# Reordered chunk steps, early first mixing pass and unrolled halves in a hybrid DeltaNet decoder block on one core

## What is computed

```python
h = x
h = h + hybrid_mixer(rms_norm(h))          # 4 gated-DeltaNet heads | 8 short-conv groups -> w_out
h = h + memory_cross_attention(rms_norm(h), rms_norm(mem))   # 256 memory tokens, 4 heads
h = h + swiglu(rms_norm(h))                # d_ff 2816
return rms_norm(h)
```

```python
v_new = u - w @ state
o     = q_dec @ state + attn @ v_new
state = state * exp(g_last) + k_dec.T @ v_new
```

## Time and profile before

| | |
|---|---|
| median of 3 runs | 3297.31 us (3297.11 to 3297.98) |
| profiled execution, own time | 3298.23 us |
| its span | 3296.5 us, 41758 instructions |
| TensorE busy | 3128.1 us (95%) |
| VectorE, ScalarE, GpSimd busy | 1200.0, 957.2, 1004.4 us (36%, 29%, 30%) |
| mean granted clock of TensorE | 0.982 |

### The profile page before, as it was taken

One profiled execution on the slowest core, in us unless ns is written; L12 is line 12 of the kernel. 1 busy time (PEld: TensorE's weight loads), 2 busy tenths in 40 slices (PEclk: granted clock), 3 DMA queues, 4 the chain that ended last, 5 costly groups with the idle time before them and its releaser, 6 DMA issues.

```text
span 3296.5 us, 41758 instructions
## 1 busy us (share of the span) xinstructions
PE 3128.1 (95%) x14926; PEld 2572.2 (78%) x14926; DVE 1200.0 (36%) x1630; ACT 957.2 (29%) x1732; POOL 1004.4 (30%) x814
## 2 busy tenths in 40 slices
PE   7899899989999999999979989998999999999998
PEld 7787677768888888888867767776888788888887
DVE  1454455546342122112235545554634311221123
ACT  3522344424232111111143234442423311111112
POOL 6322333334213332233222223333412323322332
PEclk9899999999999999999989999999999999999999
DMA  6422222132101111111132222223211111111111
GB/s 227 170 93 99 77 75 64 45 141 84 45 20 52 51 47 54 38 51 51 57 122 71 102 86 65 64 64 125 72 54 33 58 39 51 46 55 38 51 51 70
DMA packets 108410, 235.31 MB, mean 71 GB/s; under 512 B 9296, under 2 KB 50320, under 8 KB 108304
## 3 DMA queue, kind: packets, MB, share of 16 engines
q1 hardware_dynamic: 45520, 163.14, 14.7%
q10 hardware_dynamic: 62784, 70.83, 6.3%
HBM read 191.96 MB, written 41.98 MB: 71 GB/s over the span
## 4 chain that ended last, share of the span: by engine, by line
issue 45%; PE 31%; POOL 14%; DVE 4%; ACT 3%; DMA 1%; POOLq 0%; DVEq 0%; ACTq 0%; SPq 0%
POOL w_lo L1546 8%; PE PS L1995 6%; PE PS L1997 6%; PE PS L1996 6%; POOL row_lo L441 3%; PE PS L1252 2%; PE PS L1274 1%; PE PS L1232 1%; POOL heads_lo L1554 1%; DVE xn L1848 1%; PE PS L1264 1%; PE PS L1370 1%; PE PS L1305 1%; PE PS L1374 1%; PE PS L1372 1%
## 5 line engine op out<-in xcount | busy, mean ns | idle before, releaser
L1995 PE MATMUL PS<-act_hi,w_hi 128*128 128x512 f32 (+1 forms) x2496 | 983.1, 394 | 16.6 <-ACT stage L487 6.9
L1997 PE MATMUL PS<-act_hi,w_lo 128*128 128x512 f32 (+1 forms) x2496 | 958.3, 384 | 0.0
L1996 PE MATMUL PS<-act_lo,w_hi 128*128 128x512 f32 (+1 forms) x2496 | 957.4, 384 | 0.0
L1546 POOL TENSOR_TENSOR w_lo<-raw,w_hi 128x1024 fp32r<-128x1024 f32 x204 | 494.0, 2435 | 493.2 <-ACT w_hi L1625 492.3
L1995 PEld LDWEIGHTS PS<-act_hi,w_hi 128*128 128x128 f32 x2496 | 473.7, 190 | 103.6 <-issue 20.5
L1997 PEld LDWEIGHTS PS<-act_hi,w_lo 128*128 128x128 f32 x2496 | 472.6, 189 | 92.1
L1996 PEld LDWEIGHTS PS<-act_lo,w_hi 128*128 128x128 f32 x2496 | 473.7, 190 | 83.2 <-issue 1.4
L1863 DVE TENSOR_TENSOR h<-h,PS 128x1024 f32<-128x1024 f32 x272 | 332.1, 1221 | 382.0 <-PE PS L2033 345.7
L441 POOL TENSOR_TENSOR row_lo<-aa,row_hi 128x512 fp32r<-128x512 f32 x88 | 113.7, 1292 | 913.3 <-ACT row_hi L826 913.3
L1176 DVE TENSOR_TENSOR aa<-sg,PS 128x512 f32<-128x512 f32 x88 | 60.6, 688 | 880.7 <-ACT sg L822 880.7
L2029 PE MATMUL PS<-w_hi,row_hi 128*128 128x512 f32 x832 | 324.7, 390 | 0.0
(11 more groups left out here) (262 smaller groups left out, 3886.9 us busy)
## 6 DMA issues: line engine op xcount, KB each, us to landing
raw<-in_w_units SPq DMA_DIRECT2D x220, 512.0 KB, 3.3
h<-in_x SPq DMA_DIRECT2D x16, 1024.0 KB, 8.5
qkvz_d<-stage ACTq DMA_DIRECT2D x64, 256.0 KB, 2.5
raw<-att_d SPq DMA_DIRECT2D x32, 512.0 KB, 3.3
prep_raw<-in_w_units SPq DMA_DIRECT2D x16, 512.0 KB, 4.6
att_d<-product ACTq DMA_DIRECT2D x16, 512.0 KB, 3.2
qk<-qkvz_d ACTq DMA_DIRECT2D x32, 256.0 KB, 2.9
out<-result ACTq DMA_DIRECT2D x16, 512.0 KB, 4.3
```

Source lines behind the costliest of these rows:

```text
L1546: pool.tensor_tensor(w_lo[slot][:, :], raw[raw_slot][:, :], w_hi[slot][:, :].bitcast(f32), ALU.subtract)\
L1995: nc.tensor.matmul(out_ap, whi, xhi, start=start, stop=False)
L1996: nc.tensor.matmul(out_ap, whi, xlo, start=False, stop=False)
L1997: return nc.tensor.matmul(out_ap, wlo, xhi, start=False, stop=stop)
```

## The change

It consists of these parts.

1. In the chunk: TensorE makes the products of `gram` before the transposes of v, and it is these transposes that now wait for the new state. The state product goes to bank 3 (that of the new values) and not to bank 5. `am0` is made of `gram` and of a masked decay that GpSimd prepares one chunk ahead (a third product in `decays_pool`), and no longer of A. VectorE's order changes: sum of `osq` before the state; four small operations of the output norm (`output_scale`) ahead of `gram`'s products; `vb` ahead of `Xm`; the scaled outputs behind `Xe`; the taps of the short convolution from y3 to y5 to x1, x3, x4, x5, x6. ScalarE makes `rms_estimate` before `sc_rms` and `ln_norms` of y6 before its other work of y6. `FILL` of the steps w, v, o goes from 1, 1, 0 to 2, 0, 0.
2. GpSimd's subtractions of 128x1024 in the recurrence (`sq_lo`, and `split_lo` at y3 and y6) are four instructions of 128x256 each.
3. End of a half: the first two rows of mixing are loaded in step y2 of the last chunk (to another place, `mix_first`), and rounded and subtracted right behind the last chunk. TensorE starts pass 0 without the last outputs; the sums of the short convolution and the transposes of the outputs stand in pass 0 behind tile 1. SyncE issues three of the four loads of h when the state product is done, the fourth when the last output is stored. VectorE adds tile 0 between the two last normalisations.
4. GpSimd, ScalarE, VectorE and TensorE have the two halves written out instead of a loop.

```diff
--- before.py
+++ after.py
...
-FILL = [0, 0, 2, 2] + [2, 1] * 6 + [1, 1, 0]
+FILL = [0, 0, 2, 2] + [2, 1] * 6 + [2, 0, 0]
...
-        mix_first = sb("mix_first", [P, 2, D], at=[act_lo_at])
+        mix_first = sb("mix_first", [P, 2, D], at=[229344 - 8192])
...
             pool.wait_ge(S["sqh_ready"], n + 1)
             pool.wait_ge(S["nrm_full"], n)
-            pool.tensor_tensor(sq_lo[:, :, :, :].rearrange("p a h t -> p (a h t)"),
-                               rn[:, :, :, :].rearrange("p a h t -> p (a h t)"),
-                               sq_hi[:, :, :, :].rearrange("p a h t -> p (a h t)").bitcast(f32),
-                               ALU.subtract).then_inc(S["sql_ready"], 1)
+            for a in range(2):
+                for hh in range(0, NH, 2):
+                    last = pool.tensor_tensor(hflat(sq_lo[:, a, hh:hh + 2, :]),
+                                              hflat(rn[:, a, hh:hh + 2, :]),
+                                              hflat(sq_hi[:, a, hh:hh + 2, :]).bitcast(f32),
+                                              ALU.subtract)
+            last.then_inc(S["sql_ready"], 1)
...
             pool.tensor_tensor(dec[par][:, 0, :, :], dec[par][:, 0, :, :], gate("beta", m),
+                               ALU.mult).then_inc(S["decm_ready"], 1)
+            pool.wait_ge(S["decm_ready"], n * 3 + 1)
+            pool.wait_ge(S["a1t_full"], n)
+            pool.tensor_tensor(am0[:, :, :], dec[par][:, 0, :, :], over_heads(first_mask[:, :]),
                                ALU.mult).then_inc(S["decm_ready"], 1)
...
-                    split_lo((n_u + 2, 2, 2) if par == 0 else (n_u + 4, 1, 1))
+                    split_lo((n_u + 2, 2, 2) if par == 0 else (n_u + 4, 1, 1), 4)
...
-                    split_lo((n_u + 3, 0, 0))
+                    split_lo((n_u + 3, 0, 0), 4)
...
                 if step == "gram":
                     if not first:
+                        rms_estimate(act, n - 1)
                         if par == 0:
                             sc_rms(act, R - 1, 0)
-                        rms_estimate(act, n - 1)
...
+                if step == "y6" and not last:
+                    ln_norms(act, n + 1)
...
+                if step == "y2" and last:
+
+                    act.wait_ge(S["y_stored"], (half * 8 + 6) * 16)
+                    for k in range(2):
+                        load_mix(act, half, k)
...
-            act.wait_ge(S["scy_ready0"], R + 1)
-            for k in range(2):
-                load_mix(act, half, k)
+            mix_hi(act, half, 0)
+            rms_estimate(act, half * TT + TT - 1)
             sc_rms(act, R, 0)
             sc_squares(act, R, 1)
-            rms_estimate(act, half * TT + TT - 1)
-            sc_rms(act, R, 1)
+            sc_rms(act, R, 1, 6)
...
+                    if not first:
+                        output_scale(dve, n - 1)
                     dve.wait_ge(S["gram_full"], n + 1)
-                    dve.wait_ge(S["decm_ready"], n * 2 + 2)
+                    dve.wait_ge(S["decm_ready"], n * 3 + 3)
+                    dve.tensor_tensor(two(am0[:, :, :]), gram[:, :, :, 0, :], two(am0[:, :, :]),
+                                      ALU.mult).then_inc(S["am0_ready"], 1)
                     dve.tensor_tensor(two(A[:, 0, :, :]), gram[:, :, :, 0, :], two(A[:, 0, :, :]),
                                       ALU.mult).then_inc(S["a_ready"], 1)
-                    dve.wait_ge(S["a_ready"], n + 1)
-                    dve.tensor_tensor(am0[:, :, :], A[:, 0, :, :], over_heads(first_mask[:, :]),
-                                      ALU.mult).then_inc(S["am0_ready"], 1)
                 if step == "a1t":
 
+                    dve.wait_ge(S["vt_full"], n + 1)
+                    dve.wait_ge(S["vn_full"], n)
+                    dve.tensor_tensor(vb[:, :, :], r4(bank(3)), gate("beta", m), ALU.mult)\
+                        .then_inc(S["vb_ready"], 1)
                     dve.wait_ge(S["a1t_full"], n + 1)
-                    dve.wait_ge(S["vn_full"], n)
...
-                    dve.wait_ge(S["vt_full"], n + 1)
-                    dve.tensor_tensor(vb[:, :, :], r4(bank(3)), gate("beta", m), ALU.mult)\
-                        .then_inc(S["vb_ready"], 1)
+                    if not first:
+                        outputs_scaled(dve, n - 1)
...
                         sc_y_product(dve, R - 1, 1)
                 if step == "y1":
-                    if not first:
-                        normalise_o(dve, n - 1)
...
-                if par == 1 and step in ("y3", "y4", "y5"):
-                    for i, c in {"y3": ((0, 0), (1, 0)), "y4": ((2, 0), (0, 1)),
-                                 "y5": ((1, 1), (2, 1))}[step]:
-                        sc_tap(dve, R, j, c, i)
-                if par == 1 and step == "y6":
+                if par == 1 and step in ("x1", "x3", "x4"):
+                    sc_tap(dve, R, j, 0, {"x1": 0, "x3": 1, "x4": 2}[step])
+                if par == 1 and step == "x5":
+                    sc_tap(dve, R, j, 1, 0)
+                    sc_tap(dve, R, j, 1, 1)
+                if par == 1 and step == "x6":
+                    sc_tap(dve, R, j, 1, 2)
...
+                    dve.wait_ge(S["osq_ready"], n + 1)
...
+
                     dve.wait_ge(S["kv_full"], n + 1)
                     dve.wait_ge(S["s_ready"], n * 4)
                     for hh in range(NH):
                         dve.scalar_tensor_tensor(
                             state[:, hh, :], state[:, hh, :],
                             G["elast"][:, bass.ds(m, 1), hh:hh + 1].rearrange("p n h -> p (n h)"),
-                            r4(bank(5))[:, hh, :], ALU.mult, ALU.add).then_inc(S["s_ready"], 1)
...
+                            r4(bank(3))[:, hh, :], ALU.mult, ALU.add).then_inc(S["s_ready"], 1)
+
+        def end_dve(dve, half, add):
             R = half * 4 + 3
             n = half * TT + TT - 1
             sc_y_product(dve, R, 1)
+            normalise_o(dve, n)
             sc_normalise(dve, R, 3, 0)
-            normalise_o(dve, n)
+            add(0)
             sc_normalise(dve, R, 3, 1)
...
-                pe.wait_ge(S["vnew_ready"], n)
-                for hh in range(NH):
-                    t = nc.tensor.transpose(r4(bank(3))[:, hh, :], vv[:, par, hh, :], ident[:, :])
-                t.then_inc(S["vt_full"], 1)
-                pe.wait_ge(S["s_ready"], n * 4)
                 for hh in range(NH):
                     t = nc.tensor.matmul(PS[:, 5 + hh // 2, (hh % 2) * 256:(hh % 2 + 1) * 256],
                                          kqn[:, hh, 0, :],
                                          kqn[:, hh, :, :].rearrange("p s t -> p (s t)"),
                                          start=True, stop=True)
                 t.then_inc(S["gram_full"], 1)
+                pe.wait_ge(S["s_ready"], n * 4)
+                for hh in range(NH):
+                    t = nc.tensor.transpose(r4(bank(3))[:, hh, :], vv[:, par, hh, :], ident[:, :])
+                t.then_inc(S["vt_full"], 1)
...
-                    t = nc.tensor.matmul(r4(bank(5))[:, hh, :], kdec[:, hh, :], vnew[:, hh, :],
+                    t = nc.tensor.matmul(r4(bank(3))[:, hh, :], kdec[:, hh, :], vnew[:, hh, :],
...
-                        sp.wait_ge(S["oo_ready"], (half + 1) * TT)
-                        sp.wait_ge(S["y_stored"], (half + 1) * 16 * 8)
-                        sp.wait_ge(S["o_stored"], (half + 1) * 16 * TT)
...
+                        sp.wait_ge(S["vnew_ready"], (half + 1) * TT)
+                        sp.wait_ge(S["kv_full"], (half + 1) * TT)
                         for k in range(TT // 2):
+                            if k == 3:
+
+                                sp.wait_ge(S["oo_ready"], (half + 1) * TT)
+                                sp.wait_ge(S["o_stored"], (half + 1) * 16 * TT)
...
+            def split_lo(n, pieces=1):
...
+                for i in range(pieces):
+                    cs = slice(i * D // pieces, (i + 1) * D // pieces)
+                    last = pool.tensor_tensor(w_lo[slot][:, cs], raw[raw_slot][:, cs],
+                                              w_hi[slot][:, cs].bitcast(f32), ALU.subtract)
+                last.then_inc(S["w_lo_ready"], 1)
...
-            with act.Fori(0, NHALF) as half:
+            for half in range(NHALF):
...
+                    if t % 2 == 0:
+                        dve.wait_ge(S[f"h_in{t // 2}"], (half + 1) * 32)
+                    row_add(t, half * ROW_PASSES)
+
+                end_dve(dve, half, first_add)
+                for t in range(1, TT):
...
-                sc_sums(pe, half * 4 + 3, 1)
-                pe.wait_ge(S["wt_ready"], n + 1)
-                transpose_o(pe, n)
-
-
-                pe.wait_ge(S["scyn_ready"], (half + 1) * 8)
-                pe.wait_ge(S["vnew_ready"], (half + 1) * TT)
...
+                def outputs_left():
+                    pe.wait_ge(S["attn_ready"], n + 1)
+                    sc_sums(pe, half * 4 + 3, 1, 6)
```

(70 more changed lines are left out.)

26 lines of the change are left out of this document (7 added, 19 removed).

## The result

The changed kernel takes 3253.57 us, the median of four runs (3247.91 to 3254.35), beside 3297.64 us of the kernel before on the same chip: ratio 0.9862, 95% interval 0.9845 to 0.9879. That is 44 us less. The profiled execution took 3253.67 us over a span of 3251.9 us.

The account below looks back on a forecast made before the run. The prediction held that order, not work, costs: TensorE waits on chains over mostly idle VectorE and ScalarE. Terms -20.6 - 5.9 + 2.4 + 4.8 - 5.2 = -24.5 us gave 3273 us, range 3254 to 3289.

Parts of the forecast that it names:

- the earlier logarithm: Ahead of w, even chunks and chunk 0: removes TensorE's wait, but only 0.2 of 0.8 us stays gained; -1.6 us.
- Front: First transposes to y1 takes 6.0 us: odd chunks gain 1.75 us, even 1.0, chunk 0 0.3; -20.6 us.
- rival D: Front of the chunk: VectorE is late, delaying transposes of v, `vb` and y1 by 1 us; 3287 us, chance 0.08.
- Pieces and taps: y1 to w: shorter waits for `Xe` and `Xm`, partly eaten by a later `sq_lo`; -7.0 us in the recurrence.
- Rival B: Recurrence: the pieces hurt, as GpSimd goes first or `sq_lo` comes late in even chunks too; 3282 us, chance 0.14.
- Output scaling out of y1: Step y1: moving the scaling of the outputs out was not counted as a gain; 0 us.
- Tail: w to o: a second slice costs +4.0 us, the logarithm made earlier gives -1.6; together +2.4 us.
- End of a half: Mixing: pass 0 starts 8.3 us earlier, but pass 1 waits for its rows and the clock drops; +4.8 us.
- Rival C: End of a half: early mixing pays, pass 1 following pass 0 without a stop; 3252 us, chance 0.16.
- Written out: Between the halves: straight code removes the wait for the program at the jump back; -5.2 us.
- Rival E: Small loops: at new addresses their jumps back wait for the fetch, +21 to +52 us; chance 0.06.
- Start of the recurrence: Start of each half: TensorE waits for `sq_lo` itself, now in pieces; +0.55 us twice, +1.1 us.

Follow-up runs that it names:

- the two-by-two: The changed kernel with whole subtractions (3262.06 us), with the taps at y3, y4, y5 again (3251.01 us), and with both undone (3262.41 us).
- whole_and_late: The changed kernel with GpSimd's subtractions whole again and the taps back at y3, y4, y5; 3262.41 us.
- pieces alone: The kernel before with only GpSimd's subtractions cut into four pieces; 3290.78 us, ratio 0.9969 to the kernel before.
- tail_one_one: The changed kernel with one slice behind w and one behind v again, in place of two and none; 3245.54 us.
- rows_earlier: The changed kernel with units 2 and 3 of the output projection loaded before h and the second mixing pass's rows loaded earlier; 3235.42 us.
- loop_halves: The changed kernel with the two halves as one loop again on the four engines; 3259.85 us.

## Why the forecast was right in direction and short in size

The steps that failed are terms 2, 3 and 4: pieces and taps were sized too small, the scaling of the outputs was put at nothing, and the earlier logarithm was held to be eaten up by the next wait.

1. **Front** (-20.6): measured -22.0. Right, mechanism and size: 5.82 us in place of the forecast 6.0, and 6.3 to 6.4 in chunk 0. By luck two slips cancel in part: chunk 1 was counted as gaining 1.75 us like the other odd ones, but its front took 6.94 us before and it gains 1.1, while chunk 0 gains 0.6 and not 0.3. The order on TensorE alone is 16 of it. VectorE keeps up, rival D is out.
2. **Pieces and taps** (-7.0 in the recurrence): the two-by-two gives -12.0 (586.8 - 574.8). The mechanism was right, the term too small by 5. The wait for `sq_lo` that was to eat half of the gain is 0.4 us and not 1.1, because GpSimd was held up less. An odd chunk gains 1.65 us and not 1.0 (y1 to w 23.9 us in whole_and_late, 22.25 here), and even chunks gain 0.15 where I had 0. In chunk 0, where I had +0.3, y4 to y6 took 8.45 us with whole subtractions and takes 8.34. Rival B is out: pieces alone are -9.9. The Trainium skill (SBUF — State Buffer, "SBUF: two separate sides") says that of the two engines the one that starts first holds the shared ports for a whole instruction. The trace agrees: the copy takes 1.51 us beside a whole subtraction and 0.57 beside pieces. By their durations VectorE had its turn behind one piece at most.
3. **Output scaling out of y1** (not counted, 0): -7. This is the step whose mechanism failed. I followed who waits for `vb`, `Xe` and `am`, and took the scaling for work off the path. The earlier trace rows does not name it; the full list of the same view has it once, in chunk 1:

```profile
PE PS L1274 <- DVE osq L961: 0.3, 1, 0.3
```

   The starts had it: y1 to y2 took 3.80 us in chunk 3 and y2 to y3, with the same work of TensorE, 3.44; and the code has the wait of x1.
4. **Tail** (+2.4): -0.8, three parts. The slice behind w costs the 0.5 us that were forecast, but in even chunks as well as in odd ones: +7.3, less 0.8 behind v. But the earlier logarithm gives back its whole 0.9 us in even chunks and chunk 0 (-7.3), where I took 0.2, supposing that the wait for `wt` would follow. The second slice covers that wait: in tail_one_one, without it, even chunks wait there and take the same time from w to o.
5. **End of a half** (+4.8): +3.5 by the traces against the kernel before, 5.1 when taken back (-7.1 us in time, with overlapping intervals). Right, chain and sign: "nothing of the 8.3 us arrives". (The start of pass 0 adds up to 686.2, not 686.4.) The arrival of unit 2 rested on an assumed latency of 2.8 us, which no run shows by itself; by it `split_hi` was to start 27.2 us behind the state product, and it started 26.9 us behind it. Rival C, early mixing pays, is out for this kernel, and is true of rows_earlier. That its time, 3252, is near the measured 3253.57 is chance: the gain came in the recurrence, and early mixing cost time.
6. **Written out** (-5.2): 5.3 for the jump, as forecast; the other 1.8 of the -7.1 are not the loop's, since loop_halves takes 929.6 us where the kernel before takes 931.4, and their cause is open. The written-out code of chunks 0 and 7, costed at nothing, is worth about 1 us a half. The Trainium skill (Runtime: NRT & Kernel Launch, "Instruction fetch mechanics") has a taken branch wait for a fetch where its target lies outside the fetched window. The trace agrees: 8.38 us of idle time ahead of the table load with the loop against 2.92 without. Rival E, small loops that pay for their new place, is out: chunk 3 starts without a gap. (Its count was off by one: 3273 with five such stops is already 3299.)
7. **Start of the recurrence** (+1.1): +2.8, of which 0.9 is the subtraction in pieces (2.77 us in place of 2.34, twice). In the first half, another 0.7 is a later load of q, k and v (ScalarE's first square comes 7.9 us behind the gates, 7.2 before), and the sums of squares behind the longer wait take 0.63 to 0.77 us each, before 0.40 to 0.63.

Terms 2, 3 and 4 hold 15 of the missing 20 us, the written-out chunks some 2. Another 2 are the clock granted in chunk 0 of the first half, which is luck. The rest are small sums of either sign, terms 1, 5, 6 and 7 and "everything else" of the table.

Left open: why chunk 0 is granted now the lower and now the full clock; why the same code up to the gates takes 351.4 to 353.9 us, and 1 to 2 us more between the first transposes and the gates of half 1 in most of the later kernels.

## What to carry to other kernels

A list of waits names only the last releaser, and shows no short ones. Before costing a moved instruction at nothing, look up every semaphore that it raises and whose write needs the bank or buffer that it frees; here that was 7 us in 14 portions of about half a microsecond. Where VectorE is short of turns, cut GpSimd's long instructions, but not where TensorE waits for the last of them. And an earlier start of a stage is worth nothing until the chain of the next one is followed: the same early pass cost 5 us with the old queue order and paid 10 with the loads moved ahead.

## What the hardware showed unexpectedly

- Four subtractions of 128x256 in a row took 2.77 us against 2.34 whole, 0.14 us for each of the three cuts; I had assumed 3.0.
- VectorE's instructions beside pieces took 0.57 and 1.26 us in place of 1.51 and 2.91 beside whole subtractions, and 0.29 and 0.75 away from them, for the same shapes. So such a duration in a profile can be mostly the neighbour's.
- TensorE's steps in code outside inner loops can be 0.15 us shorter with the halves written out: y1 to y2 of chunk 7 takes 3.20 us, and 3.39 in loop_halves.
